# An expert layer that gathers 128 rows a token, changed to stream the whole tables against one-hot gate matrices

## The chip, the core and the metric

The kernel runs on one core of one Trainium2 chip. The metric is device microseconds of a whole execution. TensorE (PE) multiplies matrices, VectorE (DVE) and ScalarE (ACT) work on elements, GpSimd (POOL) issues the indirect transfers, SyncE (SP) issues plain ones. Sixteen DMA engines serve the core.

## The reference, cut to what matters

One inference step of one decoder layer: 1024 prompt tokens and 8 x 8 sample tokens, width 1024, all float32. The mixer (windowed attention and gated DeltaNet) comes first; then the expert layer below, a gated projection of `p`, and a last norm.

```python
def peer(x, wq, keys1, keys2, u_tab, v_tab):   # per block xb of tokens
    q = (xb @ wq).reshape(blk, PEER_HEADS, PEER_QDIM)        # 8 heads, 256 wide
    s1 = einsum('thd,hnd->thn', q[..., :half], keys1)        # 128 keys each
    s2 = einsum('thd,hnd->thn', q[..., half:], keys2)
    v1, i1 = top_k(s1, 16); v2, i2 = top_k(s2, 16)
    sc, ci = top_k(v1[..., :, None] + v2[..., None, :], 16)  # best 16 of 256 pairs
    expert = e1 * 128 + e2                                   # one of 16384
    gate = softmax(sc)
    act = gelu(einsum('td,thkd->thk', xb, u_tab[expert]))
    return einsum('thk,thkd->td', gate * act, v_tab[expert])
```

So each token uses 8 x 16 = 128 of the 16384 rows of `u_tab` and of `v_tab` (1024 floats a row, 67.1 MB a table).

## The kernel before

The program is `mixer_block`, then `peer_block`. The change touches only the second. The mixer goes over eight tiles of 128 tokens and one of 64 (the sample), and writes the hidden rows to DRAM (`h_after_mixer`). Among its matmuls, L396 (keys and values: 8 matmuls, k = 0 to 7, of 256 columns for a tile), L406 (8 of 512 columns), L474 (12 transposes of 128 x 128 for a tile) and L521 (attention times values; its 64 output rows lie in one half of PSUM's partitions for heads 0 to 3, in the other for heads 4 to 7) serve later as prices.

`peer_block` also goes tile by tile, in hardware loops (`Fori`). For a tile of 128 tokens: norm and transposes (L1411), queries with the whole `wq` held in SBUF (L1421), key scores (L1429). `best` (L1618 to L1667) finds a head's 16 experts on VectorE. GpSimd gathers, for each of the 128 slots, one row per token: a 128 x 1024 tile by an indirect transfer (L1371), through a ring of eight buffers; a buffer comes free by `used`, a row has landed by `got`. In the first part of a tile the rows come from `u`, and VectorE takes the dot products with the tokens (L1689). Then ScalarE applies gelu (L1567) and VectorE the gates. In the second part the rows come from `v`: of 16 slots VectorE adds six, weighted, to `h_cur` (L1788), and TensorE adds ten (`ON_PE`), each as a diagonal matrix made by ScalarE (L1561) times the rows (L1443, two matmuls of 512 columns). The selection for the next tile runs on VectorE between those sums. The gate of the tile before (L1462 to L1474), sigmoid, last norm and store are spread among the dot products of the current one.

The order on each engine is the order in which the code is written; engines meet in semaphores alone.

## Time and profile before

| | us |
|---|---|
| median of 3 runs | 5071.75 |
| the three runs | 5055.62, 5071.75, 12816.03 |
| profiled execution, first to last instruction (its span) | 5033.5 |
| TensorE / VectorE / ScalarE / GpSimd busy | 3032.5 / 3215.2 / 743.0 / 2595.9 |
| moved by DMA | 1207.59 MB |

For the profiled execution the page gives the span and no other time; the two lower runs lie 22.1 and 38.3 us above it. A row of the trace is one instruction or a group of like ones. "x" counts records, and "idle before" is the time in which the engine had nothing to do just before, with what ended it. The granted clock is 1.00 where TensorE ran at 2.4 GHz and 0.50 where at 1.2 GHz; between them it is a mean over the stretch.

### The profile page before, as it was taken

The numbers are of one execution on the slowest core, as the hardware profiler recorded it, in microseconds if no ns is written. First come the engines' busy times: TensorE is split into PE (matmuls) and PEld (weight loads), VectorE is DVE, ScalarE is ACT, GpSimd is POOL, SyncE is SP. The second block draws the span as 40 slices with busy tenths as digits, with TensorE's granted clock in tenths as the row PEclk, the third lists the DMA queues.
The fourth block names the chain that finished last, engine by engine and source line by source line (L and its number), as shares of the span: only waits on it lengthen the run. The fifth ranks groups of instructions, "written<-read, shape, count | busy, mean of one in ns | idle before, by whom it ended". The sixth has DMA issues, their size and how long they took to land.

```text
span 5033.5 us, 49055 instructions
## 1 busy us (share of the span) xinstructions
PE 3032.5 (60%) x13632; PEld 1920.5 (38%) x13632; DVE 3215.2 (64%) x7009; ACT 743.0 (15%) x1606; POOL 2595.9 (52%) x2511
## 2 busy tenths in 40 slices
PE   5889888987553085366447347438527546635827
PEld 4787777764442032222313223223223232222312
DVE  2444545441528877777766876776786776777672
ACT  2222222221110010011011011011101101101111
POOL 1000000000016677777777777777776777777674
PEclk9999999997576597688779679769769778867969
DMA  4000000000157799999999999999999999989986
GB/s 135 5 14 14 13 14 14 14 9 11 34 184 262 265 352 326 331 344 347 323 326 344 323 335 347 328 338 343 327 339 346 338 325 339 350 305 342 345 314 231
DMA packets 362946, 1207.59 MB, mean 240 GB/s; under 512 B 64183, under 2 KB 70871, under 8 KB 362826
## 3 DMA queue, kind: packets, MB, share of 16 engines
q0 software_dynamic: 313344, 1140.99, 63.1%
q1 hardware_dynamic: 41444, 64.96, 3.8%
q10 hardware_dynamic: 8054, 0.11, 0.1%
q8 instruction: 82, 1.34, 0.1%
q14 instruction: 22, 0.18, 0.0%
HBM read 1195.16 MB, written 11.70 MB: 240 GB/s over the span
## 4 chain that ended last, share of the span: by engine, by line
POOL 24%; issue 24%; PE 9%; DMA 8%; DVE 3%; POOLq 1%; DVEq 0%; ACT 0%; ACTq 0%; SPq 0%
POOL expert_rows L1371 23%; PE pbank L1443 8%; DMA expert_rows<-in_peer_v_dram,idx_stage 6%; DMA expert_rows<-in_peer_u_dram,idx_stage 2%; DVE expert_rows L1689 2%; POOL idx_stage L1380 2%; PE pbank L1421 1%; POOLq L1376 0%; POOLq L1370 0%; POOLq L1380 0%; PE pbank L1474 0%; DVE h_cur L1788 0%; POOLq L1366 0%; DMA g_ffn_sb<-in_norm_ffn_dram 0%; PE pbank L1470 0%
## 5 line engine op out<-in xcount | busy, mean ns | idle before, releaser
L1443 PE MATMUL pbank<-expert_rows,weight_diag 128*128 128x512 f32 (+1 forms) x2720 | 1318.2, 637 | 853.6 <-ACT weight_diag L1561 589.1
L1371 POOL DMA_INDIRECT expert_rows<-in_peer_u_dram,idx_stage x1088 | 1322.7, 1216 | 451.1 <-issue 295.7
L1689 DVE CUSTOM_DVE_ANT_0 expert_rows<-expert_rows,c_cur 128x1024 f32<-128x1024 f32 x1088 | 1321.0, 1226 | 347.7 <-DMA expert_rows<-in_peer_u_dram,idx_stage 325.1
L1371 POOL DMA_INDIRECT expert_rows<-in_peer_v_dram,idx_stage x1088 | 1143.6, 1051 | 466.2 <-issue 263.9
L1443 PEld LDWEIGHTS pbank<-expert_rows,weight_diag 128*128 128x128 f32 (+1 forms) x2720 | 520.0, 199 | 1651.9 <-issue 1284.6
L1788 DVE SCALAR_TENSOR_TENSOR h_cur<-expert_rows,weights_here,h_cur 128x1024 f32<-128x1024 f32 x408 | 524.5, 1285 | 428.7 <-DMA expert_rows<-in_peer_v_dram,idx_stage 404.1
L347 POOL MEMSET w_in_sb<- 128x4096 f32 x1 | 3.5, 3511 | 1234.1 <-PE mbank L406 1234.1
L1421 PE MATMUL pbank<-cT_sb,wq_sb 128*128 128x128 f32 x2304 | 280.0, 287 | 395.9 <-ACT pqT_sb L1515 384.6
L1421 PEld LDWEIGHTS pbank<-cT_sb,wq_sb 128*128 128x128 f32 x2304 | 277.0, 203 | 399.7 <-ACT pqT_sb L1515 385.9
L1561 ACT ACTIVATE weight_diag<-p_ident,weights 128x128 f32<-128x128 f32 x640 | 249.1, 400 | 1083.8 <-PE pbank L1443 1083.6
L1474 PE MATMUL pbank<-ple_gate_sb,cT_sb 128*128 128x512 f32 (+1 forms) x288 | 144.7, 666 | 137.5 <-DVE cT_sb L1710 137.5
L1105 DVE TENSOR_TENSOR att_sc<-att_sc,mbank 128x512 f32<-128x512 f32 (+1 forms) x168 | 102.0, 668 | 152.5 <-PE mbank L574 152.5
L376 PE MATMUL mbank<-aT_sb,w_in_sb 128*128 128x128 f32 x1536 | 182.2, 278 | 1.5 <-DVE aT_sb L920 1.5
L376 PEld LDWEIGHTS mbank<-aT_sb,w_in_sb 128*128 128x128 f32 x1536 | 177.9, 194 | 1.8 <-issue 1.8
L1462 PE MATMUL pbank<-p_ident,pqT_sb 128*128 128x128 f32 (+1 forms) x72 | 16.8, 415 | 244.4 <-DVE pqT_sb L1704 244.4
L1474 PEld LDWEIGHTS pbank<-ple_gate_sb,cT_sb 128*128 128x128 f32 (+1 forms) x288 | 59.5, 210 | 222.6 <-DVE cT_sb L1710 144.2
L1071 DVE TENSOR_TENSOR att_pT<-dn_rows,m_level 128x1024 f32<-128x1024 f32 (+1 forms) x59 | 70.7, 1198 | 114.0 <-PE mbank L561 112.5
L561 PE MATMUL mbank<-att_sc,att_pT 128*128 128x128 f32 (+1 forms) x672 | 106.9, 328 | 54.3 <-DVE att_sc L1105 30.3
L1380 POOL COPY idx_stage<-expert_all 128x8 int32 x256 | 101.1, 395 | 68.7 <-DVE expert_all L1664 67.6
L573 PE MATMUL mbank<-att_pT,att_sc 128*128 128x128 f32 (+1 forms) x672 | 131.7, 279 | 7.9 <-ACT att_pT L834 7.3
L574 PE MATMUL mbank<-att_sc,att_pT 128*128 128x128 f32 (+1 forms) x672 | 130.5, 277 | 0.0
L561 PEld LDWEIGHTS mbank<-att_sc,att_pT 128*128 128x128 f32 (+1 forms) x672 | 100.6, 239 | 58.0 <-issue 33.6
(357 smaller groups left out, 3733.0 us busy)
## 6 DMA issues: line engine op xcount, KB each, us to landing
expert_rows<-in_peer_u_dram,idx_stage POOLq DMA_INDIRECT x1088, 6.0
expert_rows<-in_peer_v_dram,idx_stage POOLq DMA_INDIRECT x1088, 6.0
wq_sb<-in_peer_wq_dram SPq DMA_DIRECT2D x2, 4096.0 KB, 21.1
w_in_sb<-in_w_in_dram SPq DMA_DIRECT2D x8, 768.0 KB, 12.3
c_nxt<-h_after_mixer SPq DMA_DIRECT2D x9, 512.0 KB, 7.4
h_cur<-h_after_mixer SPq DMA_DIRECT2D x9, 512.0 KB, 6.8
x_and_h<-in_x_prompt_dram SPq DMA_DIRECT2D x8, 512.0 KB, 3.3
dn_rT<-in_x_prompt_dram SPq DMA_DIRECT2D x8, 512.0 KB, 3.3
```

Source lines behind the costliest of these rows:

```text
L376: m = t.matmul(bank[6 + b % 2][:, c * P:c * P + r], w_in[:, k, w:w + P], aT[:, k, 0:r], start=(k == 0), stop=(k == KD - 1))
L561: m = t.matmul(bank[hh // 4][0:r, (hh % 4) * P:(hh % 4) * P + r], bt[0:r, hh, 0:r], rhs, start=True, stop=True)
L573: t.matmul(bank[b][0:r, o:o + r], xx[0:r, hh, 1, 0:r], t1[0:r, hh, 0:r], start=True, stop=True)
L574: m = t.matmul(bank[b][0:r, o + P:o + P + r], t1[0:r, hh, 0:r], xx[0:r, hh, 1, 0:r], start=True, stop=True)
L1371: g.indirect_dma_start(rows[:, k, :], None, table, bass.IndirectOffsetOnAxis(ap=stage[half][:, k:k + 1], axis=0)).then_inc(got[k], 16)
L1380: g.tensor_copy(stage[half][:, :], idx[:, bass.ds(i * SLOTS + j * STEP + half * RING, RING)]).then_inc(s["staged"], 1)
L1421: m = t.matmul(bank[4 + b % 2][:, c * P:(c + 1) * P], wq[:, k, n * P:(n + 1) * P], cT[:, k, :], start=(k == 0), stop=(k == KD - 1))
L1443: m = t.matmul(bank[c][0:r, :], diag[:, n, 0:r], rows[:, k % RING, c * 512:(c + 1) * 512], start=False, stop=False)
L1474: m = t.matmul(bank[n][0:r, :], cT[:, k, 0:r], wg[:, k, n * 512:(n + 1) * 512], start=(k == 0), stop=(k == KD - 1))
L1561: ac.activation(diag[:, n, 0:r], (fold if last else ident)[:, :], ACT.Copy, scale=wgt[:, bass.ds(j * STEP + k, 1)]).then_inc(s["diag_ready ...
L1689: v.tensor_tensor_reduce(out=rows[:, k % RING, :], in0=rows[:, k % RING, :], in1=c_cur[:, :], scale=1.0, scalar=0.0, op0=ALU.mult, op1=ALU ...
L1788: v.scalar_tensor_tensor(h_cur[:, :], rows[:, k % RING, :], w16[:, k:k + 1], h_cur[:, :], ALU.mult, ALU.add).then_inc(used[k % RING], 1)
```

## The change

`peer_block` is written anew. Tokens are taken in four groups: two tiles, two tiles, two tiles and the sample (320 tokens), two tiles. Expert e1 * 128 + e2 is row e2 of block e1, so each table is 128 blocks of 128 rows. For each group, the kernel goes through all 128 blocks of both tables in order: dot products of the block's 128 experts with all tokens of the group (`dots`), gelu, times a dense block of gates (`weigh`), and the product with the block of `v`, accumulated in PSUM over the group (`accumulate`). Nothing is gathered.

The first factor needs `u` transposed. In group 0, TensorE transposes each raw block (`turn`), ScalarE copies it to the ring, and it is also stored to DRAM, from which groups 1 to 3 read it.

The dense gates are made by the `front` of a group: norm, queries (now `wq` comes in 128-column pieces for each group), scores, `best`, softmax; then for each token a one-hot matrix of its slots' second keys, and one of the first keys times the gates, whose product (a 128 x 128 matmul) is that token's gates over all experts. Four tokens make a quad; sixteen are stored to DRAM at once, and `gblk` reads them back eight blocks at a time. The front of group g + 1 and the `gate` of group g - 1 are generators, of which each engine runs a step behind each block; numbers such as `head_at` and `quad_at` say in which block a step is due. The front of group 0 has no blocks beside it, nor has the gate of group 3. The program is unrolled: no hardware loop is left in this part.

```diff
+GROUPS = (((0, P), (P, P)), ((2 * P, P), (3 * P, P)), ((4 * P, P), (5 * P, P), (SEQ, NS)), ((6 * P, P), (7 * P, P)))
+NG = len(GROUPS)
+TMAX = max(sum(r for _, r in t) for t in GROUPS)
+TG = 16
+EB = 8
+NB = NK * NG
...
-    RING = 8
-    STEP = 16
-    ON_PE = (0, 1, 2, 3, 4, 5, 7, 9, 11, 13)
+    uT_rows = nc.dram_tensor("expert_u_transposed", [NK, P, D], F32).ap()
...
+        def head_at(g, j):
+            nt = len(GROUPS[g])
+            return 8 + 3 * nt + (5 * nt * j) // 2
...
+        def quad_at(g, k):
+            return soft_at(g) + 4 + (k * (3 if len(GROUPS[g]) == 2 else 2)) // 4
+
+        def gate_at(i):
+            return 6 + 8 * i
...
+            def load_raw(n):
+                sp.dma_start(raw[:, n % 4, :], u_tab[n * P:(n + 1) * P, :]).then_inc(u_in[n % 4], 16)
+
+            def load_v(B):
+                n = B % NK
+                sp.dma_start(v_ring[:, B % 4, :], v_tab[n * P:(n + 1) * P, :]).then_inc(v_in[B % 4], 16)
+
+            def load_gblk(c):
+                g, n = divmod(c, NK // EB)
+                nt = tokens(g) // TG
+                sp.dma_start(gblk[:, c % 2, 0:nt, :],
+                             g_rows[g][:, :, n * EB * TG:(n + 1) * EB * TG].rearrange("t e n -> e t n")).then_inc(gblk_in[c % 2], 16)
+
...
+            for p in range(-1, NB):
+                if p + 1 < NK:
+                    if p + 5 < NK:
+                        sp.wait_ge(s["t_ps"], 2 * (p + 2))
+                        load_raw(p + 5)
+                    sp.wait_ge(s["t_sb"], 2 * (p + 2))
+                    sp.dma_start(uT_rows[p + 1], u_ring[:, (p + 1) % 4, :, :].rearrange("p k n -> p (k n)")).then_inc(u_out[(p + 1) % 4], 16)
+                if NK <= p + 4 < NB:
+                    k = (p + 4) % 4
+                    if p < NK:
+                        sp.wait_ge(u_out[k], 16 * (NK // 4))
+                    sp.wait_ge(s["dots_ps"], p + 1)
+                    sp.dma_start(u_ring[:, k, :, :].rearrange("p k n -> p (k n)"), uT_rows[(p + 4) % NK]).then_inc(u_in[k], 16)
+                if p >= 2 and p + 2 < NB:
+                    sp.wait_ge(s["v_used"], p - 1)
+                    load_v(p + 2)
...
-            def gather_step(i, part, j, half, table, at):
-
-                pool.wait_ge(s["staged"], at(i, part, j, half) + 1)
-                for k in range(RING):
-
-                    pool.wait_ge(used[k], at(i, part, j, half) + 1)
-                    pool.sem_inc(s["passed"], 1)
-                    g.indirect_dma_start(rows[:, k, :], None, table,
-                                         bass.IndirectOffsetOnAxis(ap=stage[half][:, k:k + 1], axis=0)).then_inc(got[k], 16)
...
+            def load_wq(g, n):
+                N = g * 16 + n
+                if N >= 2:
+                    pool.wait_ge(s["q_ps"], N - 1)
+                pool.dma_start(wq[:, n % 2, :, :],
+                               a["peer_wq"][0, :, n * P:(n + 1) * P].rearrange("(k p) n -> p k n", p=P)).then_inc(wq_in[n % 2], 16)
...
+                for k in range(tokens(g) // TG):
+                    yield from until(cur, quad_at(g, 4 * k + 3))
+                    S = stores0[g] + k
+                    pool.wait_ge(s["gst_sb"], 4 * (S + 1))
+                    pool.dma_start(g_rows[g][k], gst[:, S % 2, :, :].rearrange("p e t -> p (e t)")).then_inc(g_out[S % 2], 16)
...
+                    for k in range(KD):
+                        m = t.matmul(bank[6][:, 0:T], wq[:, n % 2, k, :], cT[:, g % 2, k, 0:T], start=(k == 0), stop=(k == KD - 1))
+                    m.then_inc(s["q_ps"], 1)
...
+                    for n in range(4):
+                        m = t.matmul(bank[b][:, n * P:(n + 1) * P], ab[:, 1, k % 2, n, :], ab[:, 0, k % 2, n, :], start=True, stop=True)
+                    m.then_inc(s["gb_ps"], 1)
...
+            def turn(n, half):
+                if half == 0:
+                    pe.wait_ge(u_in[n % 4], 16 * (n // 4 + 1))
+                if n or half:
+                    pe.wait_ge(s["t_sb"], 2 * n + half)
+                for c in range(4):
+                    k = half * 4 + c
+                    m = t.transpose(bank[4][:, c * P:(c + 1) * P], raw[:, n % 4, k * P:(k + 1) * P], ident[:, :])
+                m.then_inc(s["t_ps"], 1)
+
+            def dots(B):
+                g, b = divmod(B, NK)
+                T = tokens(g)
+                if g == 0:
+                    pe.wait_ge(s["t_sb"], 2 * b + 2)
+                else:
+                    pe.wait_ge(u_in[B % 4], 16 * (B // 4 + 1))
+                if B:
+                    pe.wait_ge(s["gelu_done"], B)
                 for k in range(KD):
...
+                    m = t.matmul(bank[5][:, 0:T], u_ring[:, B % 4, k, :], cT[:, g % 2, k, 0:T], start=(k == 0), stop=(k == KD - 1))
+                m.then_inc(s["dots_ps"], 1)
...
-                with pe.Fori(0, steps) as j:
-                    for n, k in enumerate(ON_PE):
-                        pe.wait_ge(s["diag_ready"], (i * (SLOTS // STEP) + j) * NPE + n + 1)
-                        pe.wait_ge(got[k % RING], 16 * (at(i, 1, j, k // RING) + 1))
-                        for c in range(2):
-                            m = t.matmul(bank[c][0:r, :], diag[:, n, 0:r], rows[:, k % RING, c * 512:(c + 1) * 512],
-                                         start=False, stop=False)
-                        m.then_inc(used[k % RING], 1)
...
+            def accumulate(B):
+                g, b = divmod(B, NK)
+                pe.wait_ge(v_in[B % 4], 16 * (B // 4 + 1))
+                pe.wait_ge(s["w_ready"], B + 1)
+                if b == 0 and g:
+                    pe.wait_ge(s["acc_free"], g)
+                for i, (_, r) in enumerate(GROUPS[g]):
+                    o = offset(g, i)
+                    for n in range(2):
+                        dst = bank[2 * i + n][:, :] if r == P else bank[4][n * NS:(n + 1) * NS, :]
+                        m = t.matmul(dst, wt[:, B % 3, o:o + r], v_ring[:, B % 4, n * 512:(n + 1) * 512],
+                                     start=(b == 0), stop=(b == NK - 1))
+                m.then_inc(s["v_used"], 1)
...
+            run_out([front(0)], cur)
+            turn(0, 0)
+            turn(0, 1)
+            for g in range(NG + 1):
+                live = sides(gate, front, g)
+                for b in range(NK if g < NG else 2):
+                    B = g * NK + b
+                    if B + 1 < NK:
+                        turn(B + 1, 0)
+                    if g < NG:
+                        dots(B)
+                    if B + 1 < NK:
+                        turn(B + 1, 1)
+                    if B >= 2:
+                        accumulate(B - 2)
+                    live = step(live, cur, b)
+                run_out(live, cur)
...
+            def turn(n, half):
+                act.wait_ge(s["t_ps"], 2 * n + half + 1)
+                if n >= 4 and half == 0:
+                    act.wait_ge(s["dots_ps"], n - 3)
+                    act.wait_ge(u_out[n % 4], 16 * (n // 4))
+                ac.activation(u_ring[:, n % 4, 4 * half:4 * half + 4, :], bank[4][:, :].rearrange("p (c t) -> p c t", c=4),
+                              ACT.Copy).then_inc(s["t_sb"], 1)
+
+            def gelu(B):
+                T = tokens(B // NK)
+                act.wait_ge(s["dots_ps"], B + 1)
+                if B >= 2:
+                    act.wait_ge(s["w_ready"], B - 1)
+                ac.activation(gl[:, B % 2, 0:T], bank[5][:, 0:T], ACT.Gelu).then_inc(s["gelu_done"], 1)
...
-            def dots_of(i, j, at=turn):
-
-                for k in range(STEP):
-                    dve.wait_ge(got[k % RING], 16 * (at(i, 0, j, k // RING) + 1))
-                    v.tensor_tensor_reduce(out=rows[:, k % RING, :], in0=rows[:, k % RING, :], in1=c_cur[:, :], scale=1.0,
-                                           scalar=0.0, op0=ALU.mult, op1=ALU.add,
-                                           accum_out=dot16[:, k:k + 1]).then_inc(used[k % RING], 1)
...
+                    v.tensor_tensor(ab[:, 1, k % 2], iota[:, :].rearrange("p (o n) -> p o n", o=1).to_broadcast([P, 4, P]),
+                                    t3[:, w, 1, t0:t0 + 4].rearrange("p (t o) -> p t o", o=1).to_broadcast([P, 4, P]), ALU.is_equal)
+                    for n in range(4):
+                        m = v.tensor_scalar(ab[:, 0, k % 2, n, :], iota[:, :], t3[:, w, 0, t0 + n:t0 + n + 1],
+                                            t3[:, w, 2, t0 + n:t0 + n + 1], ALU.is_equal, ALU.mult)
+                    m.then_inc(s["ab_ready"], 1)
...
+            def weigh(B):
+                g, b = divmod(B, NK)
+                c, e = divmod(B, EB)
+                nt = tokens(g) // TG
+                if e == 0:
+                    dve.wait_ge(gblk_in[c % 2], 16 * (c // 2 + 1))
+                if B >= 3:
+                    dve.wait_ge(s["v_used"], B - 2)
+                dve.wait_ge(s["gelu_done"], B + 1)
+                v.tensor_tensor(wt[:, B % 3, 0:nt * TG].rearrange("p (a t) -> p a t", t=TG),
+                                gl[:, B % 2, 0:nt * TG].rearrange("p (a t) -> p a t", t=TG),
+                                gblk[:, c % 2, 0:nt, e * TG:(e + 1) * TG], ALU.mult).then_inc(s["w_ready"], 1)
...
-                        v.scalar_tensor_tensor(h_cur[:, :], rows[:, k % RING, :], w16[:, k:k + 1], h_cur[:, :],
-                                               ALU.mult, ALU.add).then_inc(used[k % RING], 1)
```

The order of the instructions shows the new loop. First, TensorE in the expert layer before, from the last queries of the lead-in to the first diagonal products (`weight_diag` is the diagonal, `expert_rows` the ring):

```order
L1421 MATMUL pbank<-cT_sb,wq_sb 128x128 x128
L1429 MATMUL pbank<-keysT_sb,pqT_sb 128x128 x16
L1437 MATMUL pbank<-g_ffn_sb,p_zero 128x512 x2
L1438 UNCONDITIONAL_BRANCH
L1438 ISA
L1441 ISA
L1443 MATMUL pbank<-expert_rows,weight_diag 128x512 x2
```

TensorE with the change, two blocks of group 0 while the front of group 1 makes queries (`ple_gate_sb` holds the raw u rows here, `uT_ring` the transposed ones, `weights_T` the weighted gates):

```order
L1631 MATMUL pbank<-p_ident,ple_gate_sb 128x128 x4
L1644 MATMUL pbank<-cT_sb,uT_ring 128x256 x8
L1631 MATMUL pbank<-p_ident,ple_gate_sb 128x128 x4
L1657 MATMUL pbank<-v_ring,weights_T 128x512 x4
L1555 MATMUL pbank<-cT_sb,wq_ring 128x256 x8
L1631 MATMUL pbank<-p_ident,ple_gate_sb 128x128 x4
L1644 MATMUL pbank<-cT_sb,uT_ring 128x256 x8
L1631 MATMUL pbank<-p_ident,ple_gate_sb 128x128 x4
L1657 MATMUL pbank<-v_ring,weights_T 128x512 x4
L1563 MATMUL pbank<-keysT_sb,pqT_sb 128x128 x2
```

The diagonal products are gone; every block now holds eight transposes, eight matmuls of dots and four of accumulation, and a step of the front behind them. TensorE again, two blocks of group 2, the one with 320 tokens:

```order
L1644 MATMUL pbank<-cT_sb,uT_ring 128x320 x8
L1657 MATMUL pbank<-v_ring,weights_T 128x512 x4
L1657 MATMUL pbank<-v_ring,weights_T 64x512 x2
L1644 MATMUL pbank<-cT_sb,uT_ring 128x320 x8
L1657 MATMUL pbank<-v_ring,weights_T 128x512 x4
L1657 MATMUL pbank<-v_ring,weights_T 64x512 x2
L1595 MATMUL pbank<-p_ident,en_sb 128x128 x8
```

The transposes of `u` are gone again, and two narrow matmuls for the sample tile have come.

## Rows read from the trace of the kernel before

**Rows 1.** the page: span, 40 slices; PEclk: granted clock in tenths

```profile
span 5033.5 us, 49055 instructions
...
PEclk9999999997576597688779679769769778867969
DMA  4000000000157799999999999999999999989986
```

**Rows 2.** the page, chain of waits that ended last, shares by engine

```profile
POOL 24%; issue 24%; PE 9%; DMA 8%; DVE 3%; POOLq 1%; DVEq 0%; ACT 0%; ACTq 0%; SPq 0%
```

**Rows 3.** groups by form: busy us, mean ns, idle before; GpSimd, then TensorE

```profile
L1371 POOL DMA_INDIRECT expert_rows<-in_peer_u_dram,idx_stage x1088 | 1322.7, 1216 | 451.1 <-issue 295.7 <-POOL idx_stage L1380 102.0 <-DVE dots_here L1689 45.9
...
L1443 PE MATMUL pbank<-expert_rows,weight_diag 128*128 128x512 f32 x2560 | 1240.3, 637 | 805.0 <-ACT weight_diag L1561 555.1 <-DMA expert_rows<-in_peer_v_dram,idx_stage 248.8
```

**Rows 4.** timeline where the expert layer starts and ends: start us, us, engine, line

```profile
1419.63 0.10 POOL L1348 MEMSET p_eps<- 128x1 f32 x1 [161.12 <-POOLq L52]
...
1440.89 31.40 PE L1421 MATMUL pbank<-cT_sb,wq_sb 128*128 128x128 f32 x256 [1.17 <-ACT cT_sb L1509]
...
5001.46 1.08 PE L1462 MATMUL pbank<-p_ident,pqT_sb 64*128 64x64 f32 x8 [5.35 <-DVE pqT_sb L1704]
5030.25 0.48 SPq L1342 DMA_DIRECT2D out_y_s_dram<-pqT_sb  x1
```

**Rows 5.** timeline of TensorE in the first mixer tile, 81 to 98 us

```profile
81.36 3.70 PE L396 MATMUL mbank<-w_in_sb,aT_sb 128*128 128x256 f32 x16
84.89 1.95 PE L399 MATMUL mbank<-aT_sb,w_in_sb 128*128 128x128 f32 x16
86.67 7.03 PE L406 MATMUL mbank<-w_in_sb,aT_sb 128*128 128x512 f32 x16
93.64 2.96 PE L460 MATMUL mbank<-kT_sb,qT_sb 64*128 64x256 f32 x16
96.53 1.53 PE L474 MATMUL mbank<-m_ident,cs_sb 128*128 128x128 f32 x12
```

**Rows 6.** chain of waits in order of time: start us, us, what

```profile
1779.10 10.58 PE pbank L1443 x24
```

**Rows 7.** windows: length; PE, PEld, DVE, ACT, POOL busy (count); clock, DMA share, GB/s

```profile
30.00:40.00 10.00, 0.00 (x0) 0.00 (x0) 0.00 (x0) 0.56 (x1) 0.00 (x0) 1.00 1.35 197
1426.00:1430.00 4.00, 2.50 (x12) 2.53 (x13) 0.00 (x0) 0.00 (x0) 0.00 (x0) 0.50 1.03 409
...
500.00:1000.00 500.00, 445.28 (x3111) 387.25 (x3110) 250.44 (x550) 129.17 (x271) 0.00 (x0) 0.94 0.04 14
...
1451.00:1458.00 7.00, 7.00 (x65) 7.00 (x64) 0.00 (x0) 0.48 (x1) 0.00 (x0) 1.00 0.00 0
1200.00:1230.00 30.00, 25.54 (x66) 9.13 (x67) 1.65 (x4) 3.22 (x6) 0.00 (x0) 0.82 0.02 4
...
1600.00:1650.00 50.00, 0.00 (x0) 0.00 (x0) 42.04 (x95) 0.00 (x0) 33.33 (x25) 0.50 0.68 219
```

**Rows 8.** timeline of TensorE where L521 changes to the other half of partitions

```profile
124.35 0.44 PE L521 MATMUL mbank<-att_pT,v_old_sb 128*64 128x128 f32 x4
124.56 0.44 PE L521 MATMUL mbank<-att_pT,kv_sb 128*64 128x128 f32 x4
124.84 0.38 PE L521 MATMUL mbank<-att_pT,v_old_sb 128*64 128x128 f32 x2
```

**Rows 9.** timeline of VectorE, first steps of two heads' selection (`best`)

```profile
1479.37 0.49 DVE L1623 MAX8 top_val<-cand 128x8 f32<-128x128 f32 x2
...
1488.86 0.29 DVE L1620 COPY cand<-key_scores 128x256 f32<-128x256 f32 x1 [0.19 <-issue]
```

**Rows 10.** groups by form, VectorE, then ScalarE

```profile
L1105 DVE TENSOR_TENSOR att_sc<-att_sc,mbank 128x512 f32<-128x512 f32 x160 | 99.2, 682 | 142.3 <-PE mbank L574 142.3
...
L936 DVE TENSOR_SCALAR cacc_sb<-cin_sb,conv_w_sb 128x128 f32<-128x128 f32 x96 | 20.8, 279 | 15.8 <-ACT cin_sb L731 15.8
...
L1520 ACT ACTIVATE key_scores<-pbank 128x512 f32<-128x512 f32 x36 | 18.6, 602 | 31.5 <-PE pbank L1429 31.5
```

More of the change, by code:

```diff
@@ L1343, in _ @@
+            for k in range(2):
+                sp.wait_ge(g_out[k], 16 * ((stores0[NG] + 1 - k) // 2))
             sp.wait_ge(s["y_out"], 16 * ALLT)
@@ new lines, in _ @@
+            run_out([front(0)], cur)
+            turn(0, 0)
+            turn(0, 1)
+            for g in range(NG + 1):
+                live = sides(gate, front, g)
+                for b in range(NK if g < NG else 0):
+                    B = g * NK + b
+                    if B + 1 < NK:
+                        turn(B + 1, 0)
+                    gelu(B)
+                    if B + 1 < NK:
+                        turn(B + 1, 1)
+                    live = step(live, cur, b)
+                run_out(live, cur)
@@ L1803, in _ @@
[L1803 to L1814 removed]
+                return m
@@ new lines, in add_up @@
+            def add_up(g):
+                loads = 16 * sum(1 if r == P else 2 for t in GROUPS[:g + 1] for _, r in t)
+                dve.wait_ge(s["hg_in"], loads)
+                dve.wait_ge(s["v_used"], NK * (g + 1))
+                for i, (_, r) in enumerate(GROUPS[g]):
+                    if r == P:
+                        for n in range(2):
+                            cols = slice(n * 512, (n + 1) * 512)
+                            m = v.tensor_tensor(hg[:, i, cols], hg[:, i, cols], bank[2 * i + n][:, :], ALU.add)
+                    else:
+                        m = v.tensor_tensor(hg[:, i, 0:512], hg[:, i, 0:512], bank[4][:, :], ALU.add)
+                    m.then_inc(s["h_sum"], 1)
+                dve.drain()
+                dve.sem_inc(s["acc_free"], 1)
@@ L1817, in program @@
+            run_out([front(0)], cur)
+            for g in range(NG + 1):
+                live = sides(gate, front, g)
+                for b in range(NK if g < NG else 2):
+                    B = g * NK + b
+                    if g < NG:
+                        weigh(B)
+                    if g and b == 1:
+                        add_up(g - 1)
+                    live = step(live, cur, b)
+                run_out(live, cur)
 def program(nc, a, out):
```

921 lines of the change are left out of this document (480 added, 441 removed).

## The prediction

> **What bounds the kernel now.** I read the page's slices first, then its chain of waits, then its costliest groups, and after that windows and stretches of the timeline for prices. The slices show two kernels in one: some eleven slices of mixer with the DMA engines idle and TensorE's clock at nine tenths, then the expert layer with the DMA engines at nine tenths and the clock lower [rows 1]. The chain ends through GpSimd issuing gathers (24%) and "issue" (24%); TensorE holds 9% of it [rows 2]. The groups say why: 1088 gathers of u rows, each about 1.2 us on GpSimd, as many of v rows, and VectorE and TensorE waiting in between [rows 3]. The expert layer begins at 1419.63 us of a span of 5033.5 [rows 1, 4]. So 1419.6 us stay as they are, and 3614 us are replaced.
>
> **How many TensorE instructions a matmul is.** This decides the sum. The program's accumulation issues two matmuls for each of 10 of 16 slots, 8 steps, 8 full tiles: 1280. The trace has 2560 records of that form [rows 3]. L396 is 8 matmuls (k = 0..7) for a tile and 16 records [rows 5]. An f32 matmul is therefore two records, one behind the other. A transpose is one: L474 transposes 12 blocks and has 12 records [rows 5]. Prices of one record at the full clock:
> - 512 columns: 10.58 us for 24 gives 0.441 [rows 6]; L406, 16 records from 86.67 to 93.64, gives 0.436 [rows 5]. I take 0.441, from the expert layer itself.
> - 256 columns: 81.36 to 84.89 for 16 gives 0.221 [rows 5].
> - 128 columns: 65 in 7.00 us (1451 to 1458) gives 0.108 [rows 7]. 320 columns: no row; between the two above, in proportion, 0.276.
> - a transpose: 1.53 us for 12 gives 0.128 with its tail, 0.108 without [rows 5, 7]; I take 0.12.
>
> Weight loads lie under these spacings already, since every record there has one.
>
> **What the change takes away.** All 2176 gathers, the staging copies, VectorE's 1088 dot products and 408 weighted sums, and TensorE's diagonal matmuls. All are inside the 3614 us, so nothing of them remains to be counted apart.
>
> **What it adds, per block of 128 experts** (512 blocks, 128 per group of tiles). Every token meets every expert.
> - dots (L1644), 256 tokens: 8 matmuls, 16 records x 0.221 = 3.53 us. Accumulation (L1657): 4 matmuls, 8 x 0.441 = 3.53. Block: 7.06 us. Groups 1 and 3: 128 x 7.06 = 904 us each.
> - group 0 also transposes u (L1631): 8 x 0.12 = 0.96. 128 x 8.02 = 1027 us.
> - group 2 has 320 tokens: 16 x 0.276 = 4.41, plus 3.53, plus the sample tile's two 64-wide matmuls, 4 records. These go to the two halves of bank 4's partitions. L521 passes from one half to the other at 124.35: there 8 records of 128 columns take 0.49 us (to 124.84) [rows 8], where 0.108 each would be 0.86, so neighbours in different halves run together. I take 2 x 0.441 = 0.88, block 8.82, 1129 us; without overlap 1.76, block 9.70, 112 us more. The Trainium skill, page "TensorEngine Tiling (Array Packing)", Key Properties, says that tiles of the array run in parallel but that changing the tiling mode drains the engine: by the first half the sum stands as written, by the second each block pays a switch that no row here prices.
> - the next group's front, in the gaps: queries 16 x 8 x 2 x 0.221 = 56.5; scores 64 x 0.108 = 6.9; 256 one-hot matmuls x 2 x 0.108 = 55.3; 22 transposes 2.6: 121 us for 256 tokens, 154 for 320. Three in the loop: 396 us.
> - the gate of the group before: 20 matmuls of 512 columns x 2 x 0.441 = 17.6, ten transposes 1.2, so 18.8 a tile; seven tiles in the loop: 132 us.
>
> TensorE's stream in the loop: 1027 + 904 + 1129 + 904 + 396 + 132 = 4492 us, 8.8 us a block.
>
> **What lies beside it.**
> - DMA: a block of group 0 moves raw u, v and the transposed store (0.524 MB each), gate blocks read and stored (0.131 each) and queries' weights (0.066): 1.90 MB. Plain transfers reached 409 GB/s (1426 to 1430) [rows 7], so 4.6 us under TensorE's 9. Later groups move 1.4 MB. Loads are asked for about four blocks ahead. Cost nothing.
> - VectorE: one head of one tile is 9.5 us (1479.37 to 1488.86) [rows 9]; two tiles a head in five blocks is 3.8 us a block, plus the weighting, under 0.68 [rows 10]. A quad of one-hots is 0.68 + 4 x 0.22 = 1.55 us (20.8 us / 96 for the scalar form) [rows 10], at most two a block. Under 9 us again. If TensorE's cover went, VectorE would be next, near 4.5.
> - ScalarE: copies of 128x512 at 0.52 us (18.6 / 36) [rows 10], two a block in group 0, two more for quads, a gelu that is smaller: under 3 us. dots(B+1) waits for gelu(B), since bank 5 is single; the 3.5 us accumulation stands between them. In-order engines behind a side step have two blocks of slack (three weight buffers).
>
> I add 1% of the stream for bare semaphore turns and group ends, 45 us: 4537 us.
>
> **Lead-in and tail, which nothing covers.** The front of group 0 runs alone: 30 us to the first queries (21 before, 1419.63 to 1440.89 [rows 4], plus four transfers that VectorE waits for), 15 us for queries and scores of one head on a slow clock, 16 heads x 9.5 = 152, softmax and slot transposes 8, then 64 quads. Each costs VectorE 1.55 us and TensorE, at the 0.50 granted in such stretches [rows 7], 8 x 0.216 = 1.7; with two buffers, 1.7: 108 us. Together 313 us. The tail: group 3's two tiles pass the gate one after the other. The last tile before took 28.8 us from 5001.46 to 5030.25 [rows 4], without its norm; I take 37 each and 4 for the sums: 78 us.
>
> **Sum.** 1419.6 + 313 + 4537 + 78 = 6348 us of span. The runs shown lie 22 to 38 us above the profiled span of 5033.5; with 30, **6380 us**, 26% over the median of 5071.75. Less than 2%, about 100 us either way, could not be told from no change.
>
> **Rivals.**
> - *The clock falls at the block's waits.* Every block TensorE waits at two or three places. For: the window 1200 to 1230, busy 0.85, was granted 0.82 [rows 7]. Against: the mixer, with waits of several us, kept 0.94 at 0.89 busy, and unbroken work 1.00 [rows 7]. At 0.82: 4492 / 0.82 = 5478, total 1419.6 + 313 + 5478 + 78 + 30 = 7320 us. The Trainium skill, "TensorE: Matmul & The Clock Gate", section on psum-queue depth-cycling, tells of a kernel whose small idle gaps between groups of matmuls made the clock swing; by that rule this rival holds. Chance 6%. A milder form, 0.94, gives 4779 and a total near 6620: it is in my range.
> - *Not slower: a dense f32 matmul costs one record.* If the 256 and 512 column forms of dots and accumulation went through once, the stream would be 2250 us; VectorE's 4.2 and DMA's 4.6 us a block then take over in places, some 2320 us in all, and the total is about 4160. The loop breaks even at (5033.5 - 1733 - 78) / 512 = 6.3 us a block, that is 1.4 records a matmul; only near that point would the time be the same. For: nothing but the program's own count. Against: both forms are doubled in the trace [rows 3, 5]. Chance 5%, of it 1% near the break-even.
> - *DMA becomes the bound.* The slowest stretch of plain transfers moved 197 GB/s, with short pieces (30 to 40) [rows 7]. All of group 0 at that rate: 9.6 us a block against 9.0, 90 us more; later groups stay under. So 6470 us, within the range, and short pieces are a sixth of the bytes. It would have to fall to half of that rate, 98 GB/s, to add 10 us a block in group 0 and 5 to 6 later, 3400 us, and no plain transfer here was near it. Chance 3% for anything of that kind above the range.
> - That it does not do what it says can be excluded: the order shows the dense matmuls in each block.
>
> **Numbers.** My case 86%, 6380 us. Low end: 0.436 instead of 0.441 (26), cheaper transposes (12), no bare waits (45), a lead-in 80 shorter: 6217. High end: clock 0.94 (+242) and no overlap in group 2 (+112): 6734. Range 6210 to 6730. Faster 4%, within 2% 1%, slower 95%.
>
> **What would show it.** After the lead-in: TensorE busy above 95% and a granted clock near 1.0 in every slice; 16 records of dots and 8 of accumulation in each block of about 8 to 9 us; the chain of waits mostly on L1644 and L1657; the DMA share near 0.5 in group 0 and lower later; loop start near 1733. Wrong if blocks are near 4.5 us, if the clock is under 0.9, or if TensorE waits for VectorE or for v.

## The result, and the profile after

| | before | after |
|---|---|---|
| median, us | 5063.68 (4 runs: 5039.65, 5055.62, 5071.75, 12816.03) | 6244.86 (4 runs, 6243.73 to 6246.76) |
| ratio after / before, 95% interval | | 1.2368 (1.2322 to 1.2414) |
| span of the profiled execution, us | 5033.5 | 6245.0 |
| moved by DMA, MB | 1207.59 | 848.67 |

The ratio is of undisturbed runs alone, so the one of 12816.03 us is not in it. The change makes the kernel 24% slower; 6380 was forecast, in a range of 6210 to 6730. The page after, as in [rows 1] and [rows 2]: busy time, slices of the granted clock, of DMA share and of GB/s, and the chain of waits by engine and by line.

```profile
span 6245.0 us, 65834 instructions
PE 5787.8 (93%) x25587; PEld 4002.6 (64%) x25587; DVE 1966.7 (31%) x6001; ACT 1021.0 (16%) x2041; POOL 143.3 (2%) x238
PEclk8999999867899999999999999999999999999998
DMA  4000000013276667666455556434444454455551
...
PE 72%; DVE 3%; issue 1%; DVEq 1%; DMA 0%; ACT 0%; POOL 0%; ACTq 0%; POOLq 0%
PE pbank L1644 30%; PE pbank L1657 30%; PE pbank L1583 3%; PE pbank L1555 3%; PE pbank L1631 2%; PE pbank L1621 2%; DVE onehot_ab L1917 1%; DVE onehot_ab L1914 1%; PE pbank L1563 1%; PE pbank L1612 0%; DMA ple_in_sb<-in_ple_in_dram 0%; DVE best_keys L1856 0%; PE pbank L1543 0%; DVE top_idx L1825 0%; DVE top_idx L1817 0%
```

DMA stood at nine tenths and the clock between five and nine tenths in the expert layer before; now DMA stands at three to seven tenths in the loop and the clock at nine tenths or more in every slice of it (1.00 in the windows below). The chain, which went through gathers and issue, is TensorE's for 72% of the span, and the dots (L1644) and the accumulation (L1657) hold 30% each. The dense matmuls stand first among the groups by form (as [rows 3]: busy us, mean ns, idle before):

```profile
L1657 PE MATMUL pbank<-v_ring,weights_T 128*128 128x512 f32 x4096 | 1841.2, 592 | 0.0
L1657 PE MATMUL pbank<-v_ring,weights_T 128*64 128x512 f32 x512 | 138.1, 618 | 0.0
```

4096 records for 512 blocks of four full-width matmuls: two records a matmul, as in the trace before, and no idle time in front of any of them. The loop by stage (windows; columns as in [rows 7]): lead-in, groups 0 to 3 and the tail, each cut at the first dots of a group, the last at the end of the last accumulation. Accumulation runs two blocks behind the dots, so the last two of a group lie in the next group's window: 6.9 us less for group 0, 2.2 less for group 2, 9.1 more for group 3.

```profile
1417.00:1727.68 310.68, 168.25 (x884) 139.02 (x883) 241.66 (x892) 59.64 (x113) 28.57 (x44) 0.80 0.30 107
1727.68:2837.17 1109.49, 1107.93 (x4925) 797.82 (x4924) 293.98 (x1019) 259.03 (x494) 25.73 (x37) 1.00 0.70 223
2837.17:3917.86 1080.69, 1078.83 (x4199) 735.57 (x4197) 399.86 (x1406) 152.48 (x310) 30.88 (x46) 1.00 0.55 179
3917.86:5223.12 1305.26, 1301.54 (x4531) 730.50 (x4529) 316.97 (x1039) 141.96 (x271) 28.71 (x42) 1.00 0.45 144
5223.12:6169.95 946.83, 946.72 (x3248) 609.76 (x3246) 74.47 (x158) 83.30 (x175) 5.77 (x10) 1.00 0.50 159
6169.95:6245.00 75.05, 44.45 (x100) 20.37 (x100) 14.60 (x20) 17.63 (x27) 1.81 (x3) 0.77 0.04 16
```

In the four loop windows TensorE is busy for over 99.7%, 7.2 us short of their length in all, at clock 1.00. VectorE, next in line by my reckoning, has 400 of 1081 us in the fullest of them. A block of each kind on TensorE's timeline: group 0, the last block of group 0 (which has nothing more to turn), and group 2.

```profile
2814.75 0.60 PE L1631 MATMUL pbank<-p_ident,ple_gate_sb 128*128 128x128 f32 x4
2815.19 3.62 PE L1644 MATMUL pbank<-cT_sb,uT_ring 128*128 128x256 f32 x16
2818.64 0.60 PE L1631 MATMUL pbank<-p_ident,ple_gate_sb 128*128 128x128 f32 x4
2819.08 3.60 PE L1657 MATMUL pbank<-v_ring,weights_T 128*128 128x512 f32 x8
...
2830.28 3.62 PE L1644 MATMUL pbank<-cT_sb,uT_ring 128*128 128x256 f32 x16
2833.73 3.60 PE L1657 MATMUL pbank<-v_ring,weights_T 128*128 128x512 f32 x8
2837.17 3.62 PE L1644 MATMUL pbank<-cT_sb,uT_ring 128*128 128x256 f32 x16
...
4467.50 4.58 PE L1644 MATMUL pbank<-cT_sb,uT_ring 128*128 128x320 f32 x16
4471.91 4.61 PE L1657 MATMUL pbank<-v_ring,weights_T 128*128 128x512 f32 x12
4476.45 4.57 PE L1644 MATMUL pbank<-cT_sb,uT_ring 128*128 128x320 f32 x16
```

The starts give the prices, since a record's drawn end runs past the next start. 16 records of 256 columns: 2830.28 to 2833.73, 3.45 us, 0.216 each. Eight of 512: 2833.73 to 2837.17, 3.44, 0.430 each. Four transposes: 2814.75 to 2815.19, 0.44. Blocks: 6.89 us in groups 1 and 3 (as from 2830.28 to 2837.17), 7.77 in group 0 (that and eight transposes), 8.95 in group 2 (4467.50 to 4476.45).

### The profile page after: what moved, and what is told of

It reads as the page before. It is cut to its first block, busy times and chain, and to the rows that moved or that the text cites. A ratio compares the mean times of both kernels' runs of the same rounds, so it can differ in the third digit from the quotient of the medians.

```text
span 6245.0 us, 65834 instructions
## 1 busy us (share of the span) xinstructions
PE 5787.8 (93%) x25587; PEld 4002.6 (64%) x25587; DVE 1966.7 (31%) x6001; ACT 1021.0 (16%) x2041; POOL 143.3 (2%) x238
## 2 busy tenths in 40 slices
DMA packets 372875, 848.67 MB, mean 136 GB/s; under 512 B 49863, under 2 KB 194727, under 8 KB 363850
## 4 chain that ended last, share of the span: by engine, by line
PE 72%; DVE 3%; issue 1%; DVEq 1%; DMA 0%; ACT 0%; POOL 0%; ACTq 0%; POOLq 0%
PE pbank L1644 30%; PE pbank L1657 30%; PE pbank L1583 3%; PE pbank L1555 3%; PE pbank L1631 2%; PE pbank L1621 2%; DVE onehot_ab L1917 1%; DVE onehot_ab L1914 1%; PE pbank L1563 1%; PE pbank L1612 0%; DMA ple_in_sb<-in_ple_in_dram 0%; DVE best_keys L1856 0%; PE pbank L1543 0%; DVE top_idx L1825 0%; DVE top_idx L1817 0%
## 5 line engine op out<-in xcount | busy, mean ns | idle before, releaser
L1657 PE MATMUL pbank<-v_ring,weights_T 128*128 128x512 f32 (+1 forms) x4608 | 1970.4, 595 | 0.0
L1644 PE MATMUL pbank<-cT_sb,uT_ring 128*128 128x256 f32 (+1 forms) x8192 | 1968.4, 393 | 0.0
L1644 PEld LDWEIGHTS pbank<-cT_sb,uT_ring 128*128 128x128 f32 x8192 | 1532.3, 190 | 406.6 <-issue 122.3
L1657 PEld LDWEIGHTS pbank<-v_ring,weights_T 128*128 128x128 f32 (+1 forms) x4608 | 793.7, 184 | 866.3 <-issue 832.7
L1955 DVE TENSOR_TENSOR weights_T<-gelu_out,gate_blocks 128x256 f32<-128x256 f32 (+1 forms) x512 | 226.4, 442 | 2891.3 <-ACT gelu_out L1787 2877.6
L1787 ACT ACTIVATE gelu_out<-pbank 128x256 f32<-128x256 f32 (+1 forms) x512 | 203.5, 397 | 2362.3 <-PE pbank L1644 2362.3
L1583 PEld LDWEIGHTS pbank<-onehot_ab 128*128 128x128 f32 x2176 | 269.0, 194 | 125.5 <-issue 81.0
L1583 PE MATMUL pbank<-onehot_ab 128*128 128x128 f32 x2176 | 290.2, 283 | 32.4 <-DVE onehot_ab L1917 32.3
L1917 DVE TENSOR_SCALAR onehot_ab<-iota,slots_T 128x128 f32<-128x128 f32 x1088 | 303.7, 348 | 0.0
L1555 PE MATMUL pbank<-cT_sb,wq_ring 128*128 128x256 f32 (+1 forms) x1024 | 257.2, 406 | 5.0 <-DVE enT_sb L1932 2.9
```

What stands on the lines that cost most here:

```text
L1555: m = t.matmul(bank[6][:, 0:T], wq[:, n % 2, k, :], cT[:, g % 2, k, 0:T], start=(k == 0), stop=(k == KD - 1))
L1583: m = t.matmul(bank[b][:, n * P:(n + 1) * P], ab[:, 1, k % 2, n, :], ab[:, 0, k % 2, n, :], start=True, stop=True)
L1644: m = t.matmul(bank[5][:, 0:T], u_ring[:, B % 4, k, :], cT[:, g % 2, k, 0:T], start=(k == 0), stop=(k == KD - 1))
L1657: m = t.matmul(dst, wt[:, B % 3, o:o + r], v_ring[:, B % 4, n * 512:(n + 1) * 512], start=(b == 0), stop=(b == NK - 1))
L1787: ac.activation(gl[:, B % 2, 0:T], bank[5][:, 0:T], ACT.Gelu).then_inc(s["gelu_done"], 1)
L1917: m = v.tensor_scalar(ab[:, 0, k % 2, n, :], iota[:, :], t3[:, w, 0, t0 + n:t0 + n + 1], t3[:, w, 2, t0 + n:t0 + n + 1], ALU.is_equal, ALU ...
```

## The experiments

My theory: TensorE's own stream sets the time of the loop, at two records a float32 matmul, with the clock full; everything else lies under it. Rivals: transfers or VectorE stand close behind or share in it; the clock answers to waits; the price is of the instruction and not of its type. Most experiments change one thing in the kernel after and ran once; four runs of that kernel lay within about 3 us. Where a few us matter, spans of profiled executions are compared (6245.0 for the kernel after). The two kernels with short operands ran four times each, beside seven runs of the kernel before.

### Half of the dots

```diff
-                for k in range(KD):
-                    m = t.matmul(bank[5][:, 0:T], u_ring[:, B % 4, k, :], cT[:, g % 2, k, 0:T], start=(k == 0), stop=(k == KD - 1))
+                for k in range(KD // 2):
+                    m = t.matmul(bank[5][:, 0:T], u_ring[:, B % 4, k, :], cT[:, g % 2, k, 0:T], start=(k == 0), stop=(k == KD // 2 - 1))
```

> The dots take only 4 of their 8 matmuls for each block (half of the width is left out of the dot products); loads, gates and everything else stay. Theory (TensorE's stream sets the time): 8 records of 256 columns less in 384 blocks, 8 x 0.2156 = 1.725 us each, and 8 of 320 columns in 128 blocks, about 2.2 us each: 662 + 282 = 944 us less, 6245 - 944 = 5301 us, 5290 to 5330. Rival (another engine or the transfers stand close behind): VectorE or DMA takes over in part and the time falls by less than 850 us, to above 5400.

Measured: 5324.22 us, 921 us less, 98% of the 944 that the records were worth. DMA's share in group 0 rises to eight tenths. The next waits begin to show, 3.3 us of idle before L1657 in all, where there was none, and TensorE's idle time in the four windows of the loop rises from 7.2 us to 16.7:

```profile
L1657 PE MATMUL pbank<-v_ring,weights_T 128*128 128x512 f32 (+1 forms) x4608 | 1972.4, 595 | 3.3 <-DVEq L1971 3.1
```

The stream theory holds, and there is at least that much room under it. Of the 23 us missing, 9.4 are the added idle time and 6 are the price of the dots of 320 tokens, half of which cost 2.155 us a block (half of the 4.31 us below) and not 2.2. The rest is not told apart.

### Twice the loads

```diff
+                for h, tab in enumerate((u_tab, v_tab)):
+                    if B:
+                        sp.wait_ge(twice[h], 16 * B)
+                    sp.dma_start(spare[:, h, :], tab[n * P:(n + 1) * P, :]).then_inc(twice[h], 16)
                 sp.dma_start(v_ring[:, B % 4, :], v_tab[n * P:(n + 1) * P, :]).then_inc(v_in[B % 4], 16)
```

> Each block loads its rows of u and of v once more into a spare buffer that nobody reads: 1.05 MB more for each of 512 blocks, 537 MB in all. Theory (transfers lie under TensorE): 6245 us, within 20. In group 0 the demand rises from 221 to about 343 GB/s, which is under the 409 that plain transfers reached. Rival (transfers shape the time): the share of 0.70 at 221 GB/s means a ceiling near 316 GB/s, group 0 becomes 94 us longer, 6340 us; with a ceiling of 197 GB/s, as in the slowest stretch, 1386 MB would take 7000 us of loop and the time would be above 8500.

Measured: 6245.83 us, within 1 us of the kernel after. Windows of groups 0 and 1:

```profile
1733.00:2832.00 1099.00, 1097.04 (x4877) 789.58 (x4876) 293.47 (x1018) 255.08 (x488) 25.79 (x37) 1.00 0.97 339
2832.00:3923.00 1091.00, 1089.14 (x4230) 741.65 (x4229) 400.71 (x1408) 153.30 (x312) 30.96 (x46) 1.00 0.85 302
```

The last two columns are DMA's share and GB/s. Engines that are busy for 0.97 of the window move 339 GB/s and TensorE doesn't feel it. The share of 0.70 at 223 GB/s was no sign of a ceiling at 316: the added loads raise the share by 0.27 for 116 GB/s, less for each byte than the traffic that was there, in which some two fifths of the packets are under 2 KB. So bytes, which this change cuts by 30%, were worth nothing here.

### Accumulation without lag

```diff
-                    if B >= 2:
-                        accumulate(B - 2)
+                    if g < NG:
+                        accumulate(B)
```

and VectorE's `add_up` moves ahead of the first weighting of a group.

> The accumulation of a block follows its own dots instead of those of two blocks later, so TensorE waits in each block for gelu and the weighting. From the end of the dots to the gelu 0.20 us, gelu 0.38, to the weighting 0.10, weighting 0.42, and about 0.1 back: 1.2 us a block, 512 blocks, 614 us. Theory (waits cost themselves, the clock stays): 6860 us, clock 1.00 in the loop. Rival (the clock falls at the block's waits): granted 0.82, the stream of 4442 us becomes 5417, 7830 us in all. Second rival (VectorE's and ScalarE's side steps stand in the way of gelu and weighting): the wait is 2 to 3 us in blocks with a side step, 7200 to 7500 us at clock 1.00.

Measured: 6897.85 us. Three rows of a block in group 3 (TensorE), and a window of groups 1 and 2:

```profile
6801.03 3.67 PE L1657 MATMUL pbank<-v_ring,weights_T 128*128 128x512 f32 x8 [1.10 <-DVE weights_T L1955]
6804.54 3.62 PE L1644 MATMUL pbank<-cT_sb,uT_ring 128*128 128x256 f32 x16
6809.26 3.67 PE L1657 MATMUL pbank<-v_ring,weights_T 128*128 128x512 f32 x8 [1.09 <-DVE weights_T L1955]
```
```profile
2900.00:5100.00 2200.00, 1958.11 (x7063) 1191.27 (x7062) 619.30 (x2178) 253.55 (x501) 53.88 (x77) 1.00 0.41 141
```

A block is 8.23 us (6801.03 to 6809.26), 1.34 more than with the lag: 1.10 of idle, the rest at the edges of the wait. The wait is 0.66 us in most blocks of group 0, where transposes cover part of it, 1.10 in groups 1 and 3 and 1.22 in group 2. TensorE waits in every block, is busy for 0.89 of the window, and its clock stays at 1.00. That takes away the rival of the falling clock for waits like these; it does not say that the clock stays full under any wait (see "The comparison twice"). Side steps in the way of gelu and weighting don't show either: six waits of the loop are longer than 1.3 us, the longest 5.7. By the Trainium skill, "TensorE: Matmul & The Clock Gate", its section on psum-queue depth-cycling, small idle gaps between groups of matmuls can make the clock swing; with 1.1 us of gap in 8.2 it does not here.

### The narrow pair in one half, and without it

Two experiments on the one term that rested on an overlap. In the first both narrow matmuls write to the same half:

```diff
-                        dst = bank[2 * i + n][:, :] if r == P else bank[4][n * NS:(n + 1) * NS, :]
+                        dst = bank[2 * i + n][:, :] if r == P else bank[4][0:NS, :]
...
-                                     start=(b == 0), stop=(b == NK - 1))
+                                     start=(b == 0 and (r == P or n == 0)), stop=(b == NK - 1 and (r == P or n == 1)))
```

> The sample tile's two narrow matmuls of a block both go to the same half of bank 4's partitions (their results are summed, which leaves that tile wrong). Theory (the pair runs together only because it lies in different halves): the 4 narrow records take 4 x 0.429 = 1.72 us instead of 1.12, 0.6 us more in 128 blocks: 6322 us, block of group 2 9.55 us. Rival (a narrow matmul is cheaper by itself, whatever its half): 6245 us, block 8.95.

Measured: 6356.03 us, 111 more. In the second they are left out:

```diff
+                    if r < P and 0 < b < NK - 1:
+                        continue
```

> The sample tile's two narrow matmuls are left out in 126 of the 128 blocks of group 2 (the sample's sum then lacks them). In the changed kernel their stretch lasts 1.10 us beside the eight wide records (4.53 - 3.43), and the dots behind it 4.41 where 4.30 without them in front. Theory (the two halves run together fully, 0.86, and going from full-width to half-width tiles and back costs 0.24 and 0.11): a block loses 1.21 us, 126 of them 152, 6093 us. Rival (nothing for the switch, the halves only overlap in part; the 0.11 has another cause): 126 x 1.10 = 139, 6106 us, dots still at 4.41. Both ends lie near each other; the dots' own spacing decides.

Measured: 6098.03 us, 147 less. TensorE in group 2, with the pair in one half, then without it:

```profile
4508.68 4.57 PE L1644 MATMUL pbank<-cT_sb,uT_ring 128*128 128x320 f32 x16
4513.09 5.46 PE L1657 MATMUL pbank<-v_ring,weights_T 128*128 128x512 f32 x12
4518.48 4.57 PE L1644 MATMUL pbank<-cT_sb,uT_ring 128*128 128x320 f32 x16
```
```profile
5051.27 4.47 PE L1644 MATMUL pbank<-cT_sb,uT_ring 128*128 128x320 f32 x16
5055.58 3.60 PE L1659 MATMUL pbank<-v_ring,weights_T 128*128 128x512 f32 x8
5059.02 4.47 PE L1644 MATMUL pbank<-cT_sb,uT_ring 128*128 128x320 f32 x16
```

The twelve records take 5.39 us in one half and 4.54 in two, the eight wide ones alone 3.44. So the pair costs 1.95 or 1.10: the difference, 0.85, is two records of 0.43, all that there was to overlap. 0.85 x 128 = 109 us, and by the spans the first experiment is 109.3 longer (6354.3); I had expected 0.6 x 128, having read the 0.24 us below as overlap that was missing. Of the 1.10 us, 0.86 is two records and 0.24 is left, and the dots behind the pair take 4.41 instead of 4.31. So the pair costs about 0.34 us a block beyond its records. I put that to going over to half-width tiles and back; no run has a narrow pair without such a change. The Trainium skill, "TensorEngine Tiling (Array Packing)", Key Properties, says both things, that tiles run in parallel and that changing the mode drains the engine; the 0.85 us agree with the first, and the 0.34 fit the second. I took one half of that rule and left the other unpriced. By 126 x 1.20 (8.95 - 7.75) the second experiment should have lost 151 us. Its window of group 2 is 150 us shorter (1305.3 to 1154.9); lead-in and tail were 3 us longer in that execution, so that the spans differ by 148.7 and the times by 147.

### Short operands

Only the operands of the dense products become bfloat16. SP's stores of short `u` and `v` in group 0, a conversion of `v` on ScalarE and a short copy of the tokens on VectorE are added.

```diff
+        v_ring = sb("v_ring", [P, 4, D], BF)
+        v_raw = sb("v_raw", [P, 2, D])
+        u_ring = sb("uT_ring", [P, 4, KD, P], BF)
+        cb = sb("c_short", [P, 2, KD, TMAX], BF)
...
+        wt = sb("weights_T", [P, 3, TMAX], BF)
...
+                ac.activation(v_ring[:, B % 4, :], v_raw[:, B % 2, :], ACT.Copy).then_inc(s["vr_sb"], 1)
...
+                    sp.dma_start(v_rows[p], v_ring[:, p % 4, :]).then_inc(v_out[p % 4], 16)
```

> The operands of the dense products (u transposed, v, the tokens, the weighted gates) are bfloat16; both tables are written to DRAM in bfloat16 during group 0 and read back so by groups 1 to 3. Selection, gates, transposes and all sums in PSUM stay float32. Theory (a float32 matmul costs two records of two cycles a column, 0.429 us each for 512 columns; a bfloat16 one is one record of one cycle a column, 0.215): a block of dots and accumulation takes 1.72 us instead of 6.89. Then other limits come up. Group 0 moves 1.90 MB a block, 4.65 us at 409 GB/s, 595 us; group 1: TensorE 128 x 1.72 + 209 of side work = 430 us, VectorE 401 busy, so 430 to 520; group 2: 2.3 x 128 + 160 = 455; group 3: 220 + 65 = 285. With lead-in 310, tail 75 and mixer 1417 in all about 3600 us, 3450 to 3900. Rival (the time lies in the number of instructions or in loads of weights, not in the type): the records stay near 0.2 us each or more, blocks at 4 us or above, 5000 us or more. Rival of the prediction, as an operation on real operands: one record a matmul but at the old 0.44 and 0.22 each gives about 4200.

Measured: 3870.61 us median, ratio to the kernel before 0.7653 (0.7623 to 0.7684). Dots and accumulation by form, and a stretch of group 3:

```profile
L1661 PE MATMUL pbank<-c_short,uT_ring 128*128 128x256 bf16 x3072 | 428.3, 286 | 75.4 <-ACT gelu_out L1814 39.6 <-DMA uT_ring<-expert_u_transposed 35.8
```
```profile
3770.83 1.03 PE L1677 MATMUL pbank<-v_ring,weights_T 128*128 128x512 bf16 x4
3771.70 1.04 PE L1661 MATMUL pbank<-c_short,uT_ring 128*128 128x256 bf16 x8
3772.57 1.03 PE L1677 MATMUL pbank<-v_ring,weights_T 128*128 128x512 bf16 x3
3773.43 1.04 PE L1661 MATMUL pbank<-c_short,uT_ring 128*128 128x256 bf16 x8
```

3072 records are 8 for each of 384 blocks: one a matmul. Eight of 256 columns take 0.87 us, four of 512 columns 0.87 (the third row misses one record): 0.109 and 0.217. A block is 1.74 us against 6.89, a quarter: half the records, each in half the time. The doubled record of the prediction is thus float32's, not the program's. The time is 270 us above my centre. The lead-in is not the reason (first dots at 1725.89, forecast 1727); the four groups are:

```profile
1725.89:2372.62 646.73, 513.09 (x3342) 401.27 (x3394) 294.12 (x1021) 371.77 (x621) 25.88 (x37) 0.91 1.02 376
2372.62:2919.30 546.68, 456.61 (x2616) 318.70 (x2662) 394.44 (x1410) 153.44 (x311) 31.21 (x46) 0.91 0.69 224
2919.30:3459.64 540.34, 487.14 (x2700) 295.34 (x2742) 315.03 (x1042) 142.10 (x271) 28.88 (x42) 0.96 0.74 235
3459.64:3800.46 340.82, 295.81 (x1669) 177.75 (x1698) 74.05 (x157) 83.64 (x175) 5.77 (x10) 0.95 0.78 252
```

In group 0 DMA is full at 376 GB/s (409 had been taken), and at 1.90 MB a block that is 5.05 us: 647 us instead of 595. That is 52 of the 270. Groups 1 to 3 are 72 (against the middle of 430 to 520), 85 and 56 us above their forecasts, and there no engine is full. TensorE is busy for 0.84, 0.90 and 0.87 of them, at a granted clock of 0.91 to 0.96, and waits in turn for the weighting, for gelu and for `uT_ring`. How much each of these costs was not tested.

### Short gates as well

```diff
-        ab = sb("onehot_ab", [P, 2, 2, 4, P])
+        ab = sb("onehot_ab", [P, 2, 2, 4, P], BF)
...
-        gblk = sb("gate_blocks", [P, 2, TMAX // TG, EB * TG])
-        gl = sb("gelu_out", [P, 2, TMAX])
+        gblk = sb("gate_blocks", [P, 2, TMAX // TG, EB * TG], BF)
+        gl = sb("gelu_out", [P, 2, TMAX], BF)
```

The gates in DRAM, the buffer from which they are stored and a copy of `iota` are short as well; the slots (`slots_T`) stay float32.

> As e5_short_dense, and the one-hot matrices, the dense gates and the outputs of gelu are bfloat16 too. Theory: the lead-in's 64 quads, VectorE's 1.63 us each before, fall to about 1.0, 40 us; gates' bytes halve, so group 0 moves 1.67 MB a block, 4.1 us, 70 us less; VectorE and TensorE's one-hot products shrink in groups 1 and 2, 50 to 100 us. 3450 us, 100 to 200 under e5_short_dense. Rival (VectorE's comparisons cost by their number, not by the type, and VectorE is not the bound): under 50 us less than e5_short_dense.

Measured: 3728.8 us, ratio 0.7367 (0.7335 to 0.74) to the kernel before: the fastest of all here, 142 us under the last. The gain over e5_short_dense lies in the range that was forecast, while the 3450 us rested on that kernel's forecast, which was 270 too low. It comes from other places than forecast: by the profiled executions 9 us in the lead-in instead of 40 (first dots at 1716.69 against 1725.89), 29 in group 0 instead of 70 (617.5 against 646.7), and 27, 63 and 18 in groups 1 to 3. What of it is bytes and what is cheaper one-hot products and weighting was not separated. VectorE's comparison hardly got cheaper (groups by form, first short then the kernel after):

```profile
L1947 DVE TENSOR_TENSOR onehot_ab<-iota_short,slots_T 128x512 bf16<-128x512 bf16 x272 | 185.5, 682 | 32.3 <-PE pbank L1602 21.0
```
```profile
L1914 DVE TENSOR_TENSOR onehot_ab<-iota,slots_T 128x512 f32<-128x512 f32 x272 | 188.6, 693 | 356.6 <-PE pbank L1583 332.0
```

This is not yet a comparison of types: one of its two inputs, the slots, is float32 in both. Both kernels differ from the reference in arithmetic, which is float32 throughout.

### The comparison twice

```diff
+                    v.tensor_tensor(spare[:, :, :], iota[:, :].rearrange("p (o n) -> p o n", o=1).to_broadcast([P, 4, P]),
+                                    t3[:, w, 1, t0:t0 + 4].rearrange("p (t o) -> p t o", o=1).to_broadcast([P, 4, P]), ALU.is_equal)
+                    dve.drain()
```

> VectorE makes the comparison of a quad (128 x 512, 0.69 us) twice, the first time into a spare buffer: 272 more, 187 us of VectorE in all, of it 64 in the lead-in. Theory (in the loop VectorE lies under TensorE, in the lead-in the quads are VectorE's): the lead-in grows by 64 x 0.7 = 45 us, the loop by nothing: 6290 us, the first dots at 1773. Rival (the quads of the lead-in go at TensorE's pace, as I priced both alike before): 6245 and 1728. Second rival (VectorE shapes the loop as well): 208 x 0.7 more on top, above 6400.

Measured: 6293.35 us; the first dots come at 1774.24 instead of 1727.68, 46.6 us later, and the span is 46.6 longer too (6291.6). So 64 comparisons in the lead-in count in full, and 208 in the loop, 143 us of VectorE, for nothing. The lead-in's quads are VectorE's (TensorE waits 0.47 us for `onehot_ab` in each of them in the kernel after, as in the row below); I had priced both engines nearly alike.

```profile
1718.56 1.16 PE L1583 MATMUL pbank<-onehot_ab 128*128 128x128 f32 x8 [0.47 <-DVE onehot_ab L1917]
```

These quads also show lower clocks beside waits. Windows of them in the kernel after, in this one, where TensorE waits 1.24 us in each 2.40, and in e6_short_gates, where it waits 0.89 in each 1.49 (the clock is the third number from the end):

```profile
1700.00:1720.00 20.00, 14.09 (x98) 11.62 (x96) 20.00 (x64) 7.42 (x13) 1.62 (x4) 1.00 0.39 159
1700.00:1765.00 65.00, 47.09 (x219) 40.31 (x219) 62.91 (x164) 16.18 (x28) 3.74 (x7) 0.68 0.26 109
1640.00:1660.00 20.00, 8.12 (x55) 4.48 (x52) 20.00 (x69) 8.10 (x14) 1.77 (x4) 0.50 0.26 106
```

The granted clock is 1.00, 0.68 and 0.50. It costs nothing there, since TensorE waits for VectorE in each quad even so.

### The kernel before once more

> The kernel before, unchanged, for what lies between its span and its time. Theory: nothing lies around the span in this measurement (the changed kernel shows 1.8 us); the 22 to 38 us that I read between the profiled span of 5033.5 and the runs are the scatter of the gathering kernel from run to run, so time minus span is 1 to 3 us here too. Rival: its gathers leave something after the last instruction, time minus span 20 to 40 us.

Measured: 5051.44 us with a span of 5049.6, 1.8 between them. Nothing lies around the span; what I read as a fixed cost was the scatter of the kernel before (5031.09 to 5071.16 in the seven runs beside the short kernels).

## Why the prediction was right

The step that decided, two records a float32 matmul and a stream without gaps, held. Point by point:

| term | forecast | measured |
|---|---|---|
| to the first dots | 1733 | 1727.7 |
| group 0 | 1148 | 1109.5 |
| group 1 | 1096 | 1080.7 |
| group 2 | 1288 | 1305.3 |
| group 3 | 960 | 946.8 |
| bare waits | 45 | under 10, within the rows above |
| tail | 78 | 75.1 |
| around the span | 30 | 1.8 |

The groups are the windows above; the forecasts for them are the sums of their blocks, of the next group's front and of the gates of the group before, as the prediction has them (1027 + 121; 904 + 154 + 38; 1129 + 121 + 38; 904 + 56). With each group's own accumulations, groups 0, 2 and 3 took 1116.4, 1307.5 and 937.7.

- *Where the 135 us lie.* **Record prices**: 0.430 instead of 0.441 for 512 columns (4096 records, about 47 us), 0.216 instead of 0.221 for 256 (6144, 33 us), 4.31 us instead of 4.41 for the dots of 320, 13 us, and transposes 0.11 instead of 0.12 (1024, 10 us). I took 10.58 us for 24 records from the chain [rows 6], which ends with the drawn end of a record; the rows of L406, start to start, gave 0.436 [rows 5] and were the better source. **Bare waits**: 45 us forecast; TensorE's idle time in the loop is 7.2; the 1% had no row behind it. **Around the span**: 30 us that came from scatter of the gathering kernel, read as a fixed cost.
- *What went the other way.* The narrow pair costs 1.10 + 0.10 a block, not 0.88: 40 us. The side steps of front and gates came near: 199 us in group 1 (1081 less 128 x 6.89) against 192, 160 in group 2 (1305 less 128 x 8.95) against 159.
- *Right for another reason.* The lead-in's quads were to take 108 us, by TensorE at a clock of 0.50. They take 108 (1616.65 to 1724.44), but by VectorE, 1.63 us each, while TensorE's granted clock is 1.00 in most of them. VectorE's 1.55 would have given 99, so this agreement is partly luck.
- *Beside it at no cost*: held for DMA (twice the loads; its share in group 0 is 0.70 and not near 0.5), for VectorE (twice the comparison) and, with no idle time in front of L1644 and L1657, for ScalarE. What I named next behind TensorE, VectorE near 4.5 us a block, was not: when TensorE's block fell to 1.74, it was DMA in group 0, at 5.05, and in group 1, where VectorE has most to do, VectorE was busy for 394 of 547 us.
- *The rivals.* The clock did not fall in the loop, where TensorE hardly waits, and did not under a wait in each block either. One record a matmul was seen with bfloat16, never with float32. DMA was not the bound at 1.6 times the bytes either (1386 MB).

## What to carry to other kernels

Before a sparse gather is made dense, multiply out the dense work with the records that a matmul of that type has in the trace: here 16 and 8 records a block against 128 rows a token, 4442 us of TensorE against an expert layer of 3614. A lower DMA share and a full clock are no gain by themselves. If the dense form is wanted, its operands' type decides: the same order of work was 24% slower than the gather in float32, 23% faster with short operands and 26% faster with short gates as well.
